# A two-layer decoder trunk on one core: norm sums signalled per half, KW projected between the token tiles of layer 1, two small transposes moved

## What is computed

```
proj = x @ w_in                       # 2840 columns: conv b, c, h; Q; six KV sections; 24 gates
conv_out = b_g * causal_dwconv(c_g * h)
q, kc, k_s, k_w = partial_rope(...)   # first 16 of 64 elements of each head
k_cmp, v_cmp = gelu(blocks @ w1 + b1) @ w2 + b2      # "compressed MLP" over blocks of 32 tokens
attn = g0 * attention(compressed) + g1 * attention(selected) + g2 * attention(window)
mixed = head_rmsnorm(concat(conv_out, attn))
x = layer_norm(ALPHA * x + mixed @ w_out)            # norm 1
u = causal_dwconv(x @ w_up) + bias;  val, gate = split(u)
x = layer_norm(ALPHA * x + (silu(gate) * val) @ w_down)   # norm 2
```

## Time and profile before

| what | value |
|---|---|
| runs | 680.55, 680.96, 684.35 us; median 680.96 |
| the profiled execution | 680.46 us, its span 678.6 us |
| busy, share of the span | TensorE 97%, weight loads 85%, VectorE 75%, ScalarE 55%, GpSimd 14% |
| 1 MB load, issue to landing, median | 5.2 us |

### The profile page before, as it was taken

The page is one execution under the profiler, slowest core; times in us unless marked ns, Lnnn a source line. Parts: engine busy times, 40 slices in busy tenths (PEclk is TensorE's granted clock), DMA queues, the critical chain, the costliest instruction groups (busy, mean ns, idle before and its releaser), DMA issues.

```text
span 678.6 us, 11157 instructions
## 1 busy us (share of the span) xinstructions
PE 659.3 (97%) x4290; PEld 579.8 (85%) x4290; DVE 508.9 (75%) x749; ACT 373.1 (55%) x572; POOL 94.9 (14%) x54
## 2 busy tenths in 40 slices
PE   8999999999999999999999999999999999999995
PEld 5898999769988888888778989987799888888884
DVE  4685658877997777777795555987889777777756
ACT  5674545625866666666457434563377666666620
POOL 0000012230261111110000001024116411111001
PEclk9999999999999999999999999999999999999999
DMA  9992422645775555555248252238097555555301
GB/s 288 311 301 66 145 103 90 208 138 187 249 267 185 190 199 193 198 192 171 98 126 275 96 155 96 81 107 283 28 304 254 186 186 185 186 185 185 124 0 62
DMA packets 87401, 116.81 MB, mean 172 GB/s; under 512 B 5230, under 2 KB 73536, under 8 KB 87360
## 3 DMA queue, kind: packets, MB, share of 16 engines
q1 hardware_dynamic: 85920, 111.85, 49.3%
q10 hardware_dynamic: 1440, 4.39, 1.9%
HBM read 115.19 MB, written 1.05 MB: 171 GB/s over the span
## 4 chain that ended last, share of the span: by engine, by line
PE 82%; DVE 9%; POOL 3%; ACT 1%; DMA 1%; issue 1%; SPq 0%; DVEq 0%; POOLq 0%; ACTq 0%
PE bank L1540 17%; PE bank L1293 16%; PE bank L1294 15%; PE bank L1295 15%; PE bank L1543 9%; PE bank L1376 2%; PE bank L1351 2%; DVE ring_lo L318 1%; DMA x_tok<-in_x 1%; POOL mstat L759 1%; DVE x_tok L1070 1%; DVE stats L1054 1%; PE bank L1363 1%; DVE x_tok L1052 1%; POOL mroot L761 1%
## 5 line engine op out<-in xcount | busy, mean ns | idle before, releaser
L318 DVE TENSOR_TENSOR ring_lo<-raw,ring_hi 128x2048 fp32r<-128x2048 f32 x100 | 228.0, 2284 | 20.4 <-ACT ring_hi L314 20.0
L314 ACT ACTIVATE ring_hi<-raw 128x2048 fp32r<-128x2048 f32 x100 | 190.8, 1910 | 9.4 <-DMA raw<-in_w_in 6.1
L1540 PE MATMUL bank<-xx,ring_hi 128*128 128x512 f32 x512 | 127.8, 392 | 0.0
L1540 PEld LDWEIGHTS bank<-xx,ring_hi 128*128 128x128 f32 x512 | 93.1, 189 | 17.3
L1293 PE MATMUL bank<-xx,ring_hi 128*128 128x256 f32 x320 | 94.1, 294 | 0.1
L1293 PE MATMUL bank<-ring_hi,hTh 128*128 128x512 f32 (+1 forms) x256 | 94.0, 367 | 0.0
L1294 PE MATMUL bank<-ring_lo,hTh 128*128 128x512 f32 (+1 forms) x256 | 92.8, 363 | 0.0
L1295 PE MATMUL bank<-ring_hi,hTl 128*128 128x512 f32 (+1 forms) x256 | 92.7, 362 | 0.0
L780 POOL COPY step_par<-ffn_par 128x16 f32 (+1 forms) x22 | 61.5, 2802 | 219.2 <-DVE work L1089 219.2
L1295 PE MATMUL bank<-xx,ring_lo 128*128 128x256 f32 x320 | 90.5, 283 | 0.0
L1294 PE MATMUL bank<-xx,ring_hi 128*128 128x256 f32 x320 | 90.5, 283 | 0.0
(11 more groups left out here) (190 smaller groups left out, 920.2 us busy)
## 6 DMA issues: line engine op xcount, KB each, us to landing
raw<-in_w_up SPq DMA_DIRECT2D x44, 1024.0 KB, 5.3
raw<-in_w_down SPq DMA_DIRECT2D x22, 1024.0 KB, 5.2
raw<-in_w_in SPq DMA_DIRECT2D x21, 1024.0 KB, 5.2
raw<-in_cmp_w SPq DMA_DIRECT2D x8, 1024.0 KB, 5.8
raw<-in_w_out SPq DMA_DIRECT2D x8, 1024.0 KB, 4.8
qkv<-in_ln_g ACTq DMA_DIRECT2D x4, 512.0 KB, 3.7
qkv<-in_ln_b ACTq DMA_DIRECT2D x4, 512.0 KB, 5.0
raw<-in_w_in SPq DMA_DIRECT2D x2, 512.0 KB, 5.3
```

What stands on the lines that cost most here:

```text
L314: nc.scalar.activation(ring_hi[slot_of(L, u)][:], raw[raw_of(L, u)][:], ACT.Copy).then_inc(hi_done, 1)
L318: eng.tensor_tensor(ring_lo[slot_of(L, u)][:], raw[raw_of(L, u)][:], ring_hi[slot_of(L, u)][:].bitcast(fp32), ALU.subtract).then_inc(split ...
L1540: pe.matmul(dst[:], wh[:, k, P * c:P * (c + 1)], xx[:, k].rearrange("p a n -> p (a n)"), start=k == 0, stop=False)
```

## The change

The signals `y1_done` and `y2_done` for the first token tile are raised once for each column half, and each half's residual waits for its own. In layer 1, KW of tile 0 is projected before Q of tile 1, with the transposes of x for tile 1 behind its fifth step of eight; VectorE makes the low halves of unit 3 and of KW before the last residual of layer 0, ScalarE copies KW of tile 0 before Q of tile 1, and `kw_turn` gives the count that `rope` and the conv units wait for. In both layers the first `transpose_hidden` stands behind the first 12 matmuls of conv unit 9, the second behind `scores_pair(2)`. No arithmetic is added or taken away.

```
@@ -287,6 +287,10 @@
         def xT_turn(L, t, b):
             return 4 * L + (2 * t + b if L else t + 2 * b) + 1
+
+        def kw_turn(L, t):
+
+            return 6 * L + (3 + 3 * t if L else 5 + t)
         def out_unit_of(k):
@@ -639,6 +643,8 @@
                 copy_q(L, 0)
                 split_hi(act, L, 5)
                 copy_kv(L, 0)
+                if L:
+                    copy_kw(L, 0)
                 copy_q(L, 1)
                 split_hi(act, L, 6)
                 split_hi(act, L, 7)
@@ -650,7 +656,8 @@
...
                 split_hi(act, L, 8)
-                copy_kw(L, 0)
+                if L == 0:
+                    copy_kw(L, 0)
                 split_hi(act, L, 9)
                 copy_kw(L, 1)
                 split_hi(act, L, 10)
@@ -841,7 +848,7 @@
             def rope(L, t, chain):
-                dve.wait_ge(qkv_copied, 6 * L + 5 + t)
+                dve.wait_ge(qkv_copied, kw_turn(L, t))
...
@@ -1045,7 +1052,7 @@
             def residual(L, which, t, n, banks, chain):
                 if t + n < 2:
-                    dve.wait_ge(y1_done if which == 0 else y2_done, 2 * L + t + 1)
+                    dve.wait_ge(y1_done if which == 0 else y2_done, 3 * L + 2 * t + n + 1)
                 else:
                     unit_used(dve, L, out_unit_of(KT - 1) if which == 0 else NU - 1)
...
@@ -1120,6 +1127,12 @@
                     if u:
                         split_lo(V, *u)
+            def split_kw_lo(L):
+                dve.wait_ge(hi_done, L * NU + 5)
+                for (hi, lo), src in kw_pieces(L):
+                    ins = V.tensor_tensor(lo, src, hi.bitcast(fp32), ALU.subtract)
+                ins.then_inc(split_done[raw_of(L, 4)], 1)
+
             chain = Chain(dve, dve_seq)
             for L in range(DEPTH):
                 if L == 0:
@@ -1134,12 +1147,9 @@
                     split_lo(V, L, 2)
                     split_lo(V, L, 3)
                     masks()
+                    split_kw_lo(L)
                 else:
                     x_low(L, XT_BANK, 1, xT_hi, xT_lo[1])
-                dve.wait_ge(hi_done, L * NU + 5)
-                for (hi, lo), src in kw_pieces(L):
-                    ins = V.tensor_tensor(lo, src, hi.bitcast(fp32), ALU.subtract)
-                ins.then_inc(split_done[raw_of(L, 4)], 1)
                 for u in (5, 6, 7, 8):
                     split_lo(V, L, u)
                 dve.wait_ge(par_ready, L + 1)
@@ -1278,11 +1288,11 @@
                 if L + 1 < DEPTH:
                     x_low(L + 1, XT_BANK, 0, xT_hi, xT_lo[0])
                     split_lo(V, L + 1, 2)
+                    split_lo(V, L + 1, 3)
+                    split_kw_lo(L + 1)
                 residual(L, 1, 1, 1, FFN_BANK, chain)
                 moments(L, 1, 1, chain)
                 centre(L, 1, 1, chain)
-                if L + 1 < DEPTH:
-                    split_lo(V, L + 1, 3)
                 normalise(L, 1, 1, x_ready, chain)
@@ -1321,7 +1331,7 @@
                 if part == 0 and half in (None, 0):
                     wait_unit(L, u)
                     if idx < 2:
-                        pe.wait_ge(qkv_copied, 6 * L + 5 + idx)
+                        pe.wait_ge(qkv_copied, kw_turn(L, idx))
                     elif idx in (2, 4):
                         pe.wait_ge(c_copied, 2 * L + idx // 2)
                     else:
@@ -1592,9 +1602,10 @@
                     pe.wait_ge(h_lo, H_CREDIT + L * STEPS + s + 1)
                     for n in range(2):
                         ins = piece(s, 0, n)
+                        if s == final:
+                            ins.then_inc(y2_done, 1)
                     if s == mid:
                         piece(first, 1, 0)
-                ins.then_inc(y2_done, 1)
                 piece(mid, 1, 0)
                 piece(final, 1, 0).then_inc(y2_done, 1)
                 free_unit(piece(first, 1, 1), L, NU - STEPS + first)
@@ -1619,10 +1630,29 @@
                     transpose_x(L, x_ready, XT_BANK, 0, xT_done, (0,))
                     keep_busy(bank[7], 6)
+                wide = 256 + NGATE
+                kw_hi, kw_lo = (r[slot_of(L, 4)][:, 0:(KT - 1) * wide].rearrange("p (k n) -> p k n", k=KT - 1) for r in (ring_hi, ring_lo))
+
+                def project_kw(t):
+                    if t == 0:
+                        wait_unit(L, 4)
+                    tok = slice(P * t, P * (t + 1))
+                    for k in range(KT):
+                        if L and t == 0 and k == KT - 3:
+                            transpose_x(L, x_ready, XT_BANK, 1, xT_done)
+                        hi, lo = (kw_hi[:, k, :], kw_lo[:, k, :]) if k < KT - 1 else (kw_last[:, 0, :], kw_last[:, 1, :])
+                        ins = mm3(bank[4 + t][:, 0:wide], xh[:, k, tok], xl[:, k, tok], hi, lo, k == 0, k == KT - 1)
+                    if t:
+                        free_unit(ins, L, 4)
+                    else:
+                        ins.then_inc(proj_done, 1)
+
                 in_order = [(t, first, b) for t in range(TT) for first in (0, 2) for b in range(2)] if L else \
                     [(t, first, b) for first in (0, 2) for b in range(2) for t in range(TT)]
                 for t, first, b in in_order:
                     tok = slice(P * t, P * (t + 1))
+                    if L and t and first + b == 0:
+                        project_kw(0)
                     u = first + b
                     if t == 0:
                         if L == 0 and u < 2:
@@ -1647,8 +1677,6 @@
                         ins.then_inc(proj_done, 1)
                     if L + t + u == 0:
                         transpose_x(L, x_ready, XT_BANK, 1, xT_done, (1,))
-                    elif L and t == 0 and u == 2:
-                        transpose_x(L, x_ready, XT_BANK, 1, xT_done)
                 pe.wait_ge(par_in, 16 * 8 * (L + 1))
                 settled(pe)
@@ -1657,18 +1685,8 @@
...
-                wait_unit(L, 4)
-                wide = 256 + NGATE
-                wh, wl = (r[slot_of(L, 4)][:, 0:(KT - 1) * wide].rearrange("p (k n) -> p k n", k=KT - 1) for r in (ring_hi, ring_lo))
-                for t in range(TT):
-                    tok = slice(P * t, P * (t + 1))
-                    for k in range(KT):
-                        hi, lo = (wh[:, k, :], wl[:, k, :]) if k < KT - 1 else (kw_last[:, 0, :], kw_last[:, 1, :])
-                        ins = mm3(bank[4 + t][:, 0:wide], xh[:, k, tok], xl[:, k, tok], hi, lo, k == 0, k == KT - 1)
-                    if t:
-                        free_unit(ins, L, 4)
-                    else:
-                        ins.then_inc(proj_done, 1)
+                for t in range(L and 1, TT):
+                    project_kw(t)
                 for part in range(2):
                     conv_unit(L, 0, part)
@@ -1700,15 +1718,16 @@
                 pe.wait_ge(masks_ready, 2)
                 scores_pair(L, 0)
                 cmp_hidden(L, 0)
+                conv_unit(L, 2, 0, 0)
                 transpose_hidden(L, 0)
-                for part in range(2):
-                    conv_unit(L, 2, part)
+                conv_unit(L, 2, 0, 1)
+                conv_unit(L, 2, 1)
                 cmp_k(L)
                 cmp_hidden(L, 1)
                 transpose_p(L, 0)
+                scores_pair(L, 2)
                 transpose_hidden(L, 1)
-                scores_pair(L, 2)
                 transpose_p(L, 1)
                 conv_unit(L, 3, 0)
                 cmp_v(L)
@@ -1776,7 +1795,7 @@
                 for c in range(2):
                     for k in (2, 3):
                         ins = out_product(L, 0, c, k)
-                ins.then_inc(y1_done, 1)
+                    ins.then_inc(y1_done, 1)
                 for k in range(4):
                     out_product(L, 1, 0, k)
                 for k in range(2):
```

48 lines of the change are left out of this document (22 added, 26 removed).

## The result

| | before | after |
|---|---|---|
| median of the runs shown with the result (22 each) | 680.64 us | 676.79 us |
| lowest of them | 680.32 us | 676.42 us |
| profiled execution, its span | 680.46, 678.6 us | 676.75, 674.9 us |
| TensorE busy | 659.3 us | 658.6 us |
| start of the last matmul | 670.16 us | 666.93 us |

The ratio of the times is 0.9941, with a 95% interval from 0.9924 to 0.9957: the medians are 3.85 us apart. The forecast was 676.5, the measured median is 0.3 above it. Lines of the kernel after are numbered some ten higher: `mm3` is L1303 to L1305 (L1293 to L1295 before), `transpose_x` L1324, `transpose_hidden` L1407, `transpose_p` L1373, the residual L1059, the low part of x L846.

A forecast was written before the change was run, and what follows sets the result against it. TensorE, busy 97% of the span at its upper clock, was taken as the bound; only its stalls and the tail could be won. 1.9 + 1.9 + 0.5 = 4.3 off 680.46 gives 676.2, forecast as 676.5 us, range 675.2 to 679.2.

The forecast's parts named there:

- Norm 1's signals: Layer 1's first norm 1 residual stands behind `scale_heads` in VectorE's queue, so an earlier signal gains 0.
- Norm 2 between the layers: Half signals run VectorE's chain 1.02 us earlier at the layer boundary; layer 1's first projection gains 0.60 us.
- The new order: Layer 1's reordering removes stalls of 1.22 and 0.26 us at the second tile's transposes; 0.17 comes back.
- The 0.17: Wait expected behind the second tile's transposes: x's low part usable at 354.65, the KW matmuls ending at 354.4 to 354.5.
- Hidden transposes: Moving both in the attention stage gains 0.71 and 0.31 less 0.05 us per layer: 1.9, bounds 1.4 and 2.05.
- The 0.05 for `maxima` 2: Charge per layer for the moved second transpose delaying `maxima` 2 and the exponentials; bounds 0 and 0.3 us.
- Tail: Behind the last matmul, the product rather than VectorE's own chain releases the last residual: 0.50 us.
- (a): Gain given back downstream in later stalls such as `heads_T` and `conv_roots`: 679.4 us, partly 678.3; chance 0.12.
- (b): Nothing at the boundary: VectorE's new splits delay the second tile's chain, a new wait replacing the old: 678.0 us; chance 0.11.
- (c): Second tile's low part and KW hang on one late chain; loses from 4.7 us late, 684.3 at 8; chance 0.04.
- (d): Moved transposes let TensorE's clock fall for ten microseconds, losing some 5 us: about 681.5 us; chance 0.03.
- (e): Half signals bring nothing because something else releases VectorE; 0.60 and 0.50 stay out: 677.6 us; chance 0.08.

The follow-up runs named there:

- r3_best: r1 with norm 1's first two residuals ahead of `scale_heads(1)`, split 20 behind it, x1's transposes one step earlier: 670.06 us.
- r0: Kernel before with convolution and head roots freed (epsilon added on VectorE, pause before its next split): 676.63 us.
- r1: Kernel after with the same freed roots (epsilon added on VectorE, pause before its next split): 672.77 us.
- e6_late2: Kernel after with two unused filler reductions on VectorE ahead of layer 0's last residual: 680.51 us in one execution.
- e1: Kernel before with only the signals per half: 688.81 us beside 689.51 of before, ratio 1.0003.
- e6_late7: Kernel after with six unused filler reductions on VectorE ahead of layer 0's last residual: 688.31 us in one execution.
- e4: Kernel after with the second hidden transpose back ahead of `scores_pair(2)`: 680.99 us in one execution, with two long powers.
- a0: The kernel after run again, unchanged, beside the kernel before on one chip: 678.76 us against 682.50.
- e5: Kernel after with both hidden transposes issued twice: 677.29 us in one execution.
- e3: Kernel before with only layer 1's new order: 686.62 us beside 689.51 of before, ratio 0.9973.
- b1: Kernel after with norm 1's first two residuals earlier on VectorE, x1's first transposes one step earlier: 679.89 us, ratio 0.9898 to before.

## Why the prediction was right, and where it was not

**Norm 1's signals: 0.** Held. Layer 1's first residual of norm 1 starts at 470.92 with VectorE busy to its start, as in the earlier trace rows. r3_best adds the condition: once the residual stands ahead in VectorE's queue, the early signal is worth using.

**Norm 2 between the layers: 0.60.** 0.71 measured. The row at 332.04 that the prediction calls the second half's residual is the first half's, which the signal behind both halves had held back; the second half's starts at 333.37. The 1.02 us of the chain do not hang on the name. The residual's start was right: 330.48, where 331.02 less the 0.52 us by which TensorE is ahead by then makes 330.50. The low part of x was foreseen at 338.6 and came at 338.03, that is 338.55 by the old clock; the 0.83 from its start to TensorE's was 0.91 (338.03 to 338.94), but TensorE, which I took to be the later at 339.57, reached it at 339.46 by the old clock: the four transposes and their change of form take 0.35 (338.59 to 338.94), not 0.41.

**The new order: 1.22 and 0.26, less 0.17.** The two stalls went. With the 0.71 the stage gave 2.11 instead of 1.91, inside the bounds of 1.0 and 2.2. The 0.17 did not come back as a wait: the low part starts at 353.13, and the first matmul of Q that reads it stands 0.13 behind the last of KW (353.78, 353.91). The chain has 0.27 us of room instead of 0.35, and the cover of 1.5 us for the loads held: no wait for the rotary step or a weight appears in TensorE's list.

**Hidden transposes: 2 x 0.97, put at 1.9.** This is the term that was mis-sized; 2 x 0.62 and 2 x 0.01 came, 1.26 in all, below its lower bound of 1.4. The step that failed is "less a step of 0.12" and "less the 0.41 of four transposes": what I subtracted was the steady step of one form, while a transpose of 30 rows stands 0.21 behind a 256-column matmul, and 0.31 behind a mask matmul, even when its input is there: ScalarE's copies end at 390.91 and 403.84 in after, 0.95 and 1.99 before the pairs. So 0.83 - 0.21 = 0.62 was to be had at the first, and of the second's 0.31 next to nothing. The 0.05 for `maxima` 2 did not arise: from unit 3 to the transposes that wait for the exponentials it is 4.70 us in both kernels (409.71 to 414.41, 406.47 to 411.17). But the delay behind it is real. In after:

```profile
408.39 0.68 DVE L923 TENSOR_REDUCE smax<-bank 128x4 f32<-128x512 f32 x1
...
410.60 0.21 ACT L532 ACTIVATION_READ_ACCUMULATOR probs<-bank,nmax 128x1 f32 x1
```

`maxima` 2 starts 1.92 behind unit 3's first matmul, and in before 0.24 (409.71 to 409.95): 1.7 us later, where 1.2 was foreseen. The exponentials end at 410.81, 0.36 before TensorE wants them. The rule cited there, from the Trainium skill, TensorE: Matmul & The Clock Gate, section Architectural detail, that VectorE takes its instructions strictly in order, agrees with these rows: the maxima stayed behind `hidden(1)`. The delay cost nothing, with 0.36 us to spare.

**Tail: 0.50.** The traces give 0.47.

**Sum.** 2.11 + 2 x 0.62 + 2 x 0.01 + 0.47 = 3.84, less 0.09 in layer 0, where the wait at `times_v(8)` grew (its distance from 0.83 to 0.92): 3.75. The span fell by 3.7 (678.6 to 674.9), and 4.3 was forecast. That the median, 676.79, came out 0.3 above the forecast and not 0.55 is luck. I added 0.3 because the three runs that I had of before had their median 0.5 above the profiled execution; with 22 runs it is 0.2 above (680.64), and what drew some runs up, the long powers, I didn't know of.

**The rivals.** (a) The gain is given back downstream: only those 0.09; in layer 1 TensorE's lead of 3.25 us behind the compressed attention is 3.22 at the last matmul. r0 and r1 exclude that the gain came out of the waits for the roots. (b) New stall at the boundary: no, with 0.27 us to spare. (c) The mechanism is real, its price was too low. I had the change losing from 4.7 us of lateness on; by the one execution of e6_late2 it has lost everything at 2.25, since 1.8 us of slower clock came with a stall of 2 us. (d) The clock: not by transposes. In no trace did the sixteen at the boundary let it fall, not even with the stall of 1.64 us in e1; idle time of 2 us and more did, at the boundary of e6_late2 and e6_late7 and behind seven of the ten long powers. The sentence of the Trainium skill, TensorE: Matmul & The Clock Gate, section Part 4: PE-mode transpose, that transposes do not count as busy as matmuls do, is neither borne out nor refuted: the granted clock is 1.00 where the eight stand together, but they take only 0.81 us there. (e) The half signals bring nothing: true of them alone to the extent of 0.44 of 0.72 (e1), not in the change.

## What to carry to other kernels

A stall read as "distance less the steady step" is only a stall if the two instructions have one form; take the distance of the same two forms from a place where nothing waits. An earlier signal is worth what the next wait lets through, so look for the edit that removes that wait and try the two together. And when times scatter, compare the durations of one small instruction over several traces before trusting a median: here each of two powers of 128x8 elements, 2.1 us longer or not, moved a kernel's time by 2.1 to 4.4 us, and the whole change is worth 3.9.

## What the runs showed of the hardware

- **A split on VectorE holds up GpSimd, by who is first.** GpSimd's power takes 1.63 or 1.64 us when it starts 0.09 or 0.10 us ahead of VectorE's two-input subtraction, and 3.74 when the two start within 0.01 us of each other: it then ends 1.50 behind the end of the subtraction, which takes 2.24. The addition that starts 0.28 behind a subtraction ends 0.06 to 0.15 behind its end (128.24 and 128.30 in after, 128.05 and 128.20 in e4). The subtraction never got longer (2.24 to 2.29). The Trainium skill, SBUF — State Buffer, section SBUF: two separate sides, says that the two engines share a port pair that one holds for a whole instruction while the other blocks, also against a VectorE instruction with two inputs in SBUF. The rows agree where VectorE is first or level; where GpSimd is first they differ: the subtraction that starts 0.09 behind the power does not wait for its 1.64.
- **What 2.1 us there cost.** In e4 two long powers moved the last matmul by 4.3 us with the clock at 1.00; in e1, where it fell behind both, by 8.5 although 0.3 was gained at the boundary, so some 4.4 each. Of the 17 times of before beside a0, six are 680.3 to 680.6, four 681.4 to 682.5, six 685.3 to 685.9 and one is 690.67: one long power at the upper clock would make 682.4, two 684.6 to 689.1 (estimates from 680.3 and the costs in e4 and e1), which leaves some of them unexplained. Which power was long in an execution that was not profiled can't be seen.
- **Changing form.** Going from 256-column matmuls to two 30-row transposes and back costs some 0.3 us beside the 0.12 of the transposes (e5). Why is open.
- **TensorE's clock.** The upper level was kept through stalls of 1.2 and 1.64 us at the boundary (before, e1). It fell behind the one stall there of 2.0 and the one of 6.5 us (0.59 and 0.50 in the windows behind them), and behind seven of ten stalls of 2.55 at `conv_roots`. e4, twice, and e6_late7 kept it through these, where e1 to e3, twice each, and b1 lost it; what decides between them is not settled.
